# Expert up-projections with the weights stationary and the tokens moving, and a gather that skips empty slots

## The reference, cut to what matters

```
def expert_block(args):
    xi, e = args                                   # xi (128, 1024)
    return (jax.nn.silu(xi @ w1[e]) * (xi @ w3[e])) @ w2[e]
    # w1, w3: (1024, 512), "up"; w2: (512, 1024), "down"
```

## Time and profile before

| | before |
|---|---|
| median of 3 runs | 2293.46 us (2292.86 to 2296.08) |
| profiled execution | 2291.61 us, span 2289.9 us |
| PE busy | 2038.0 us, 89% of the span |
| DVE busy | 1416.0 us, 62% |
| ACT busy | 1079.6 us, 47% |
| bytes moved by DMA | 356.16 MB, of which 273.27 MB on SP's queue |
| granted TensorE clock, mean | 0.955 of full speed |

### The profile page before, as it was taken

How to read it: one execution, slowest core, us unless ns; L and a number is a source line. 1 busy time by engine, 2 the same in 40 slices (tenths; PEclk the granted TensorE clock), 3 DMA queues, 4 the chain that set the end, 5 groups by cost and what they waited for, 6 DMA issues and landing times.

```text
span 2289.9 us, 31459 instructions
## 1 busy us (share of the span) xinstructions
PE 2038.0 (89%) x12278; PEld 1273.3 (56%) x12278; DVE 1416.0 (62%) x1864; ACT 1079.6 (47%) x1525; POOL 290.8 (13%) x335
## 2 busy tenths in 40 slices
PE   4999999899988787899899989999469999999991
PEld 3455465566644454788645875568435544444440
DVE  5455633688863475755433264543559999999976
ACT  4472223455545331110333353433248888888873
POOL 1010000000000563243021000000010111111102
PEclk9999999899999897999999999999779999999995
DMA  7111112111001134212311142040459999999986
GB/s 274 38 51 33 28 38 59 48 42 52 19 24 41 60 126 114 84 56 56 132 53 47 52 125 74 19 156 14 166 208 423 422 422 422 422 422 422 422 327 229
DMA packets 138212, 356.16 MB, mean 156 GB/s; under 512 B 37968, under 2 KB 91376, under 8 KB 111472
## 3 DMA queue, kind: packets, MB, share of 16 engines
q1 hardware_dynamic: 94304, 273.27, 31.4%
q10 hardware_dynamic: 34944, 48.24, 6.1%
q0 software_dynamic: 8848, 33.03, 3.7%
HBM read 305.74 MB, written 44.56 MB: 153 GB/s over the span
## 4 chain that ended last, share of the span: by engine, by line
PE 52%; DVE 7%; issue 2%; DMA 1%; ACT 1%; POOL 1%; ACTq 0%; POOLq 0%; DVEq 0%
PE psum L1084 22%; PE psum L709 20%; PE psum L960 1%; PE psum L1073 1%; DVE arena L2128 1%; DVE arena L2125 1%; PE psum L947 1%; PE psum L1012 1%; PE psum L1037 1%; PE psum L728 1%; PE psum L955 1%; PE psum L1102 1%; PE psum L1050 1%; PE psum L972 0%; POOL arena L2580 0%
## 5 line engine op out<-in xcount | busy, mean ns | idle before, releaser
L709 PE MATMUL psum<-arena 128*128 128x512 f16 (+2 forms) x6000 | 1021.0, 327 | 15.5 <-ACT arena L1249 10.1
L709 PEld LDWEIGHTS psum<-arena 128*128 128x128 f16 x6000 | 576.4, 99 | 390.1 <-issue 24.8
L1084 PE MATMUL psum<-arena 128*128 128x512 f16 x2304 | 514.6, 383 | 16.5 <-issue 9.5
L668 DVE SCALAR_TENSOR_TENSOR arena<-arena 128x2048 f16<-128x2048 f32 x192 | 437.8, 2287 | 78.9 <-ACT arena L663 78.7
L663 ACT ACTIVATE arena<-arena 128x2048 f16<-128x2048 f32 x192 | 365.5, 1908 | 66.0 <-DMA arena<-in_w_dram 36.8
L1084 PEld LDWEIGHTS psum<-arena 128*128 128x128 f16 x2304 | 225.2, 99 | 283.9 <-issue 22.6
L1744 DVE SCALAR_TENSOR_TENSOR arena<-arena 128x512 f16<-128x512 f32 (+1 forms) x212 | 140.7, 684 | 171.1 <-ACT arena L1231 171.0
L1231 ACT ACTIVATE arena<-arena 128x512 f16<-128x512 f32 (+1 forms) x212 | 126.4, 615 | 58.3 <-PE psum L709 11.1
L2441 POOL TENSOR_TENSOR arena<-arena 128x512 f32<-128x512 f32 x48 | 64.7, 1348 | 621.4 <-DVE arena L1767 621.4
L1249 ACT ACTIVATE arena<-psum,arena 128x512 f32<-128x512 f32 x64 | 43.7, 683 | 196.3 <-PE psum L709 188.5
L2565 POOL DMA_INDIRECT arena<-xhat,arena x32 | 63.6, 1988 | 508.1 <-PE psum L1073 447.0
(11 more groups left out here) (362 smaller groups left out, 2300.8 us busy)
## 6 DMA issues: line engine op xcount, KB each, us to landing
arena<-in_w_dram SPq DMA_DIRECT2D x192, 1024.0 KB, 11.9
arena<-in_merge_w_dram SPq DMA_DIRECT2D x64, 256.0 KB, 3.1
yrows<-arena ACTq DMA_DIRECT2D x32, 512.0 KB, 7.9
arena<-in_w_in_dram SPq DMA_DIRECT2D x48, 256.0 KB, 2.8
gdn_lq<-arena ACTq DMA_DIRECT2D x8, 1024.0 KB, 4.3
arena<-gdn_lq ACTq DMA_DIRECT2D x8, 1024.0 KB, 4.9
arena<-in_xattn_wkv_dram SPq DMA_DIRECT2D x32, 256.0 KB, 3.0
yrows<-arena POOLq DMA_DIRECT2D x1, 7680.0 KB, 31.4
```

What stands on the lines that cost most here:

```text
L668: nc.vector.scalar_tensor_tensor(half_of(XW[m][1], half), half_of(XLAND[m], half), WS, half_of(XW[m][0], half), ALU.mult, ALU.subtract).th ...
L709: mm = nc.tensor.matmul(bank[prt[0]:prt[1], c0:c1], lhs[a](k), rhs[b](k), start=(k == 0 and a + b == 0), stop=(k == nk - 1 and a == 1))
L1084: mm = nc.tensor.matmul(PS[:, bank, :], left[a][:, k, :], right[b][:, k, columns], start=k + a + b == 0, stop=(k == n - 1 and a == 1))
```

## The change

Three things are changed together.

1. `make_hi` and `make_lo` of w1 and w3 (not w2) write `XW` in another order. The source is read as it lies, 2048 elements a partition in a row; element 4q+k goes to position k*512 + (its number among those of the same k). So neighbours in the source land 1024 bytes apart (512 f16 elements), four times, then the pattern moves on by 2 bytes. `make_lo` also reads hi in that order.
2. `up` makes the weights stationary (128 x 128, contiguous in the new order) and moves 128 tokens: 8 slices x 4 groups of inner units x 3 passes x 2 matrices, 192 matmuls of 128x128. The result has inner units on partitions already, so `g_tr` is gone, and both `g_copy` read `GU` from SBUF instead of PSUM. They now wait for down(e-1) themselves.
3. The index table is turned round (2T minus the old value), so that an empty slot gives 2048, and the gathers have a bound of 1023 beyond which a row is skipped.

```diff
+        def arrived(m, half):
+            w = half_of(XLAND[m], half)
+            return w if m == 2 else w.rearrange("p t (q k) -> p (t q) k", k=KE)
+        def by_group(m, s, half):
+            w = half_of(XW[m][s], half)
+            return w if m == 2 else w.rearrange("p a b -> p (a b)").rearrange("p (k n) -> p n k", k=KE)
...
-            nc.scalar.activation(half_of(XW[m][0], half), half_of(XLAND[m], half), ACT.Copy, scale=WS).then_inc(w_hi[m], 1)
+            nc.scalar.activation(by_group(m, 0, half), arrived(m, half), ACT.Copy, scale=WS).then_inc(w_hi[m], 1)
...
-            nc.vector.scalar_tensor_tensor(half_of(XW[m][1], half), half_of(XLAND[m], half), WS, half_of(XW[m][0], half),
+            nc.vector.scalar_tensor_tensor(by_group(m, 1, half), arrived(m, half), WS, by_group(m, 0, half),
                                            ALU.mult, ALU.subtract).then_inc(w_lo[m], 1)
...
-                product(2, XT[s], XW[0], 0, e, slice(0, DE), pe_a1)
-                product(3, XT[s], XW[1], 1, e, slice(0, DE), pe_a3)
-            def g_tr(e):
-                pe.wait_ge(vec_g, e + 1)
-                after(pe, vec_gt, e)
-                gs = GU.rearrange("p (q k) -> p k q", k=KE)
-                for k in range(KE):
-                    tr = nc.tensor.transpose(PS[:, 4, k * P:k * P + P], gs[:, k, :], ident)
-                tr.then_inc(pe_gt, 1)
+                for m, done in ((0, pe_a1), (1, pe_a3)):
+                    for k in range(KT):
+                        if k % (KT // 2) == 0:
+                            pe.wait_ge(w_lo[m], 2 * e + 1 + 2 * k // KT)
+                        half, t = divmod(k, KT // 2)
+                        for f in range(KE):
+                            fs = slice(f * P, f * P + P)
+                            for a, b in ((0, 0), (0, 1), (1, 0)):
+                                mm = nc.tensor.matmul(PS[:, 2 + m, fs], half_of(XW[m][a], half)[:, f, t * P:t * P + P], XT[s][b][:, k, :],
+                                                      start=k + f + a + b == 0, stop=(k == KT - 1 and f == KE - 1 and a == 1))
+                    mm.then_inc(done, 1)
...
             def g_copy(e):
-                act.wait_ge(pe_gt, e + 1)
-                S.activation(GUT[0], PS[:, 4, :].rearrange("p (k n) -> p k n", k=KE), ACT.Copy).then_inc(act_gt, 1)
+                act.wait_ge(vec_g, e + 1)
+                after(act, pe_y, 2 * e)
+                S.activation(GUT[0], GU.rearrange("p (k n) -> p k n", k=KE), ACT.Copy).then_inc(act_gt, 1)
...
-            then(V.tensor_copy(IDX, PS[:, 6, 64:64 + NBLK]), "index")
+            then(V.tensor_scalar(IDX, PS[:, 6, 64:64 + NBLK], -1.0, float(2 * T), ALU.mult, ALU.add), "index")
...
-                G.indirect_dma_start(XR[e % 2], None, XH_D, bass.IndirectOffsetOnAxis(IDX[:, e:e + 1], 0)).then_inc(rows_in[e % 2], 16)
+                G.indirect_dma_start(XR[e % 2], None, XH_D, bass.IndirectOffsetOnAxis(IDX[:, e:e + 1], 0), bounds_check=T - 1,
+                                     oob_is_err=False).then_inc(rows_in[e % 2], 16)
```

More of the change, by code:

```diff
@@ L623, in build @@
         y_out = [sem(f"y_out{s}") for s in range(2)]
-        pe_xt, pe_a1, pe_a3, pe_gt, pe_y = (sem(f"expert_pe_{n}") for n in ("xt", "a1", "a3", "gt", "y"))
+        pe_xt, pe_a1, pe_a3, pe_y = (sem(f"expert_pe_{n}") for n in ("xt", "a1", "a3", "y"))
         pe_used = (pe_a1, pe_a3, pe_y)
@@ L1117, in period @@
                     down(e - 1)
-                g_tr(e)
             def block_beyond(e, j):
@@ L2317, in g_mul @@
                 dve.wait_ge(pe_a3, e + 1)
-                after(dve, pe_gt, e)
+                after(dve, act_gt, e)
+                after(dve, vec_gt, e)
                 V.scalar_tensor_tensor(GU, PS[:, 3, :], GSCALE / WS, SL, ALU.mult, ALU.mult).then_inc(vec_g, 1)
@@ L2329, in g_copy @@
                 dve.wait_ge(act_gt, e + 1)
-                V.tensor_tensor(GUT[1], PS[:, 4, :].rearrange("p (k n) -> p k n", k=KE), GUT[0], ALU.subtract).then_inc(vec_gt, 1)
+                after(dve, pe_y, 2 * e)
+                V.tensor_tensor(GUT[1], GU.rearrange("p (k n) -> p k n", k=KE), GUT[0], ALU.subtract).then_inc(vec_gt, 1)
             def period(e, s, n):
@@ L2555, in _ @@
                             .then_inc(*po.mark("iota", o_))
-                    G.iota(K_INT[:, 80:88], pattern=[[P, TT]], base=0, channel_multiplier=1).then_inc(*po.mark("iota_tok"))
+                    G.iota(K_INT[:, 80:88], pattern=[[-P, TT]], base=2 * T, channel_multiplier=-1).then_inc(*po.mark("iota_tok"))
                     G.iota(K2_INT[:, 0:NBLK + 1], pattern=[[P, NBLK + 1]], base=0, channel_multiplier=0).then_inc(*po.mark("iota_blk"))
@@ L2574, in _ @@
                     with pool.If(number > j):
-                        G.indirect_dma_start(XR[0], None, XH_D, bass.IndirectOffsetOnAxis(IDX[:, NE + j:NE + j + 1], 0)).then_inc(rows_in[0], 16)
+                        G.indirect_dma_start(XR[0], None, XH_D, bass.IndirectOffsetOnAxis(IDX[:, NE + j:NE + j + 1], 0),
+                                             bounds_check=T - 1, oob_is_err=False).then_inc(rows_in[0], 16)
                         pool.wait_ge(y_out[0], 16 * NE // 2 + 16 * (j + 1))
```

## The result

| | before | after |
|---|---|---|
| median | 2294.77 us (2292.86 to 2309.74, 4 runs) | 3271.54 us (3266.18 to 3275.69, 4 runs) |
| ratio to before | | 1.420 (95% interval 1.414 to 1.426) |
| profiled execution, its span | 2291.61, 2289.9 us | 3268.62, 3266.9 us |
| mean granted clock | 0.955 | 0.822 |

The changed kernel is 42% slower. I had forecast 2520 us, with 2385 to 2640 as the range: slower, as it came, but by 228 us where it is 977.

What follows compares the result with a forecast made beforehand. DMA was taken to set the pace at 17.36 us a period; after the change the ring, with jumps and clock, would take 24.7. 31 x (24.7 - 17.36) = 228 us, 2291.6 + 228 = 2520 us; range 2385 to 2640.

Steps and rivals of the forecast that it cites:

- The ring: Chain up, one hi, three lo, x_copy, next up: 16.70 us before, 24.7 us a period forecast after the change.
- my clock term: At the head of a1, after PE's pause, half clock loses 1.6 to 2.5 us a period; 2.0 taken.
- The price of a jump: Each hi or lo conversion of w1 and w3 takes 1.45 us more; 5.80 us for four in the ring.
- the upper end: Most a jumping conversion could add: 2.9 us for lo if both its streams pay, 1.45 for ACT.
- lower end: Least a jumping conversion could add: 0, if f16 writes go into a buffer that hides the jump.
- My signs: Right: hi and lo of w1 and w3 about 3.4 and 3.7 us, DMA near 300 GB/s; wrong: conversions below 2.4 us.
- The rule on jumping results: Skill's DVE rule: a result jumping at every element costs 1.71 instead of 1.05 ns; lo between 3.65 and 4.2 us.
- Expert 0's early conversions at nothing: Expert 0's four conversions fall where PE is full and DVE and ACT wait for it: cost 0.
- Up with narrow matmuls: 128-column matmuls of up take 56 ns each, so up costs 10.75 us instead of 10.36.
- the rival: Narrow matmuls come every 81 ns by a load not hidden behind 128 columns: ring 26.6 us, 2578 us; chance 5%.
- The gather: Skipped empty slots save 0.26 MB a period, DMA 16.8 instead of 17.4 us; worth nothing at 24.7 us a period.
- w2 and the rest: w2's conversions stay as before; g_copy's new wait adds nothing; the last g_tr, 0.5 us, is left out.

Runs made afterwards that it cites:

- m_jumps: Separate program that only converts 128x2048 blocks in eight forms on each engine; the change's order took 9251 to 9.3 us-class times: DVE 9252 ns, in a row 2293.
- hi_row: Changed kernel, but hi of w1 and w3 is written in a row while lo still jumps (products not the layer's); 3111.11 us.
- lo_row: Changed kernel, but lo of w1 and w3 is written and reads hi in a row while hi still jumps (products not the layer's); 3134.71 us.
- row_writes: Changed kernel with the conversions' two inner loops swapped: results written in a row, source read every 16 bytes; 2562.25 us, ratio 1.113.
- step_loads: Changed kernel, but conversions write in a row and up reads its stationary weights with a step of four columns; 2311.03 us, ratio 1.0016.
- skip_only: Kernel before with only the turned index table and the bound of the gathers; 2311.25 us, ratio 1.0014.
- step_full: step_loads with the full gathers of the kernel before, so no skipped rows; 2303.61 us, ratio 0.999.
- spread2_skip: skip_only with filled slots spread over all places of a block and results written by two transfers of 64 places; 2292.28 us, ratio 0.998.
- spread2_step: step_loads with filled slots spread over all places of a block and results written by two transfers of 64 places; 2311.6 us, ratio 1.0035.

## Why the prediction was wrong in size, step by step

*The ring.* Right. All but 1.4 of PE's 868.0 us of idle time ahead of up end with DVE's x_copy. My formula with measured durations, 16.90 + 7.39 (hi) + 3 x 6.95 (lo), gives 45.1 us, and 47.05 were measured; the 1.9 left is about my clock term of 2.0.

*The price of a jump.* This step failed. The period came out 47.05 - 24.7 = 22.35 us longer than forecast, and (7.39 - 1.45) + 3 x (6.95 - 1.45) = 22.4 of it is this price, so it makes some 31 x 22.35 = 693 us of the 749 missing. I took 1.45 us for each conversion, from L2131 and L2133 and L2128, and called 2.9 us the upper end. The price is 7.4 us on ACT and 6.95 on DVE. The rows were read correctly, but they are f32 and DVE's: m_jumps gives 0.65 to 0.68 ns an element there for a source and for f32 results (0.9 on ACT). I had named the difference in type only as a reason why f16 might be cheaper (the "lower end"). I put no end on the other side, where a lone f16 result costs 3.4 to 3.6 ns more than one in a row. My signs show the same gap: for conversions they had "wrong" only below 2.4 us, and 9.3 lies on the side without one. DMA near 300 GB/s (150 measured) and PE idle some 6 us (27.8) followed from the price.

Two smaller choices inside the step held: lo pays for one of its two jumping streams only (9252 against 9251 ns), and ACT, for which I had no row, pays about as DVE does (7.4 against 6.95 us; for f32 results or a source that jumps a third more, 1.8 to 1.9 against 1.3 to 1.4).

*The rule on jumping results.* The Trainium skill, "Vector Engine (DVE) Microarchitecture Reference", section 5.2, which measured 4-byte elements, gives 1.71 ns for a jumping result. By 2048 elements that is 3.5 us; the trace has 3681 ns for f32 results, in agreement, and 9251 for f16 ones, which it doesn't cover.

*Expert 0's early conversions at nothing.* This failed too: 54.5 us, "where PE is full with work of its own and DVE and ACT wait for it". They are eight instructions of 9.3 us, the first of ACT's at 1532.66 and the last of DVE's at 1630.16, in a stage where each engine in turn holds up the next. The whole stretch that rows 5 show a part of, and the second of the five pieces that it has in the changed kernel:

```profile
1519.17 84.00 PE L709 MATMUL psum<-arena 128*128 128x256 f16 x768 [1.46 <-issue]
```

```profile
1552.43 17.29 PE L719 MATMUL psum<-arena 128*128 128x256 f16 x144 [11.04 <-DVE arena L1782]
```

PE now stands still four times, 44.0 us in all, each time for DVE's L1782, which comes behind a conversion. The four pieces of 144 matmuls after these pauses take 72.4 us where 109.4 ns each make 63.0: 9.4 more, at a clock that starts at half (0.50 from 1552.4 to 1554 us). With the 1.1 us by which the stretch starts later that is 54.5. hi_row and lo_row confirm it: with DVE's four jumping alone up(0) is 24.7 us later than before, with ACT's alone 28.8. The cover was real at 1.9 us and nearly so at 3.8: in row_writes up(0) starts at 1677.68, only 2.4 us later than before.

*Sum of both:* 693 + 54 = 747 of the 749 us between 2520 and 3268.6.

*Up with narrow matmuls.* Right. In the changed kernel's stretch at full clock 95 of them take 5.47 us, 57.6 ns each with the tail of the last one; over the 192 of step_loads it is 56.7. I had 56, and the rival 81.

*Clock.* Right in size. Windows at the start of the same up:

```profile
2624.00:2625.00 1.00, 0.62 (x7) 0.62 (x8) 1.00 (x2) 0.29 (x2) 0.00 (x0) 0.50 1.07 221
...
2627.00:2628.00 1.00, 1.00 (x20) 1.00 (x18) 1.00 (x1) 1.00 (x2) 0.00 (x0) 0.94 0.92 324
```

After the pause of 27.8 us PE starts at the half level, 1.2 GHz, and is at the full one again 2.7 us later; at the next up it takes 4.4. Over all periods up takes 12.1 to 13.7 us where it needs 10.75, so 1.4 to 3.0 us are lost, 2.4 in the mean (2.0 forecast).

*The gather.* "Worth nothing" came true, and for the reason given: at 150 GB/s DMA does not set the pace. What I added, that the 0.26 MB a period are worth 0.6 us where DMA does set it, is wrong: in skip_only they bring nothing.

*w2 and the rest.* Right: 2.29 and 1.91 us as before, and step_full shows that g_tr, the waits of g_copy and the stationary weights sum up to nothing.

The range failed with the price. A sum over a ring that holds one uncertain duration four times can be no better than that duration, and mine had its upper end from rows of another type.

## What to carry to other kernels

When an instruction is made to write f16 results apart from each other, price it by a row of that type or measure it alone: here the same jump cost DVE 0.7 ns in f32 and 3.4 ns in f16. Keep pairs together (1079 ns against 1056 in a row on ACT), put the jump on the source (3.8 us against 9.3), or, best here, leave it to the weight load, which read columns 8 bytes apart at no cost (10.88 us for 192). And an instruction that grows four- to fivefold has to be looked up wherever it occurs, for what covered 1.9 us elsewhere won't cover 9.3.

## What the runs showed that I had not expected

- An f16 result that jumps costs some 4.5 ns on ACT and on DVE alike (9294 and 9251 ns for 2048); on ACT, where steps were tried, an element costs 1.3, 2.4 and 4.6 ns at 4, 8 and 16 bytes (1335, 2472 and 4731 ns for 1024).
- Small instructions were slower beside such conversions: in the changed kernel L2335 takes 785 ns in the mean, 684 before, and L1667, ACT's x_copy, 761, 584 before. It is the engine's own conversion that does it, not the other's: in hi_row, where only DVE jumps, they take 884 and 584 ns, in lo_row, where only ACT does, 682 and 749. Two jumping conversions at once slow each other by 1% only (9382 against 9294 ns).
- Rows that an indirect gather skips gave no time back: 8.39 MB fewer, POOL's packets 20 us shorter, the same DMA share, and a rate of 393 to 417 GB/s instead of 422.
- PE's clock in the router stage, where nothing was changed, is not always the same. The stretch in the kernel before and in step_loads:

```profile
1616.00:1630.00 14.00, 14.00 (x131) 14.00 (x130) 2.64 (x4) 6.36 (x13) 0.00 (x0) 1.00 0.94 345
```

```profile
1616.00:1630.00 14.00, 14.00 (x69) 14.00 (x68) 2.94 (x4) 3.26 (x6) 0.00 (x0) 0.50 0.58 195
```

  PE is busy all the time in both, after a pause, at the full level in the one and at the half level in the other, and up(0) starts at 1675.24 us and at 1693.31. skip_only and step_full have 0.50 there too, spread2_skip 0.83 and spread2_step 0.94. What decides between them wasn't tried.
